# Root scales moved behind the matmuls, and the modulation sums divided between VectorE and GpSimd with ScalarE

## The chip, the core and the metric

The kernel runs on one core of a Trainium2 chip. The metric is the device time of one execution in microseconds (us). Times inside the kernel are read from one profiled execution, counted from the start of its span.

## The reference, cut to what matters

Four transformer-like layers run one after another on 512 tokens of width 1024 (the last two also on 256 context tokens). What the change touches:

```python
def rms_norm(x, g):
    y = xf * lax.rsqrt(jnp.mean(xf * xf, axis=-1, keepdims=True) + NORM_EPS)
    return (y * g).astype(x.dtype)

# first block, layers 0 and 1
h = rms_norm(x, attn_norm[0]);  q, k, v = split(h @ w_qkv)       # then attention with 8 heads
x = x + attention(...) @ w_o
x = x + swiglu(rms_norm(x, ffn_norm[l]), w_gate_up[l], w_down[l])  # (silu(g) * u) @ w_down
k, v = split(rms_norm(x, kv_norm) @ w_kv);  q = rms_norm(x, attn_norm[1]) @ w_q

# second block, layers 0 and 1: the modulation
m = silu(cond) @ w_mod + b_mod         # for cond = c and for cond = c_ctx; 6 x 1024 outputs each
h = rmsnorm(x, norm) * (1 + scale) + shift
```

`h @ w` is `root(token) * ((x * gain) @ w)`, since the root is one number for each token. `w_mod` is read once for each layer (24 MB) and serves both conditionings.

## The kernel before

The activations X lie with features on the partitions: 8 tiles of 128 features x 512 tokens. Weights come in blocks of 128 output features; each block (128 x 1024 values, 512 KB) is loaded to `w_raw`, rounded by ScalarE to `w_hi` (L568), and what rounding left is computed by VectorE as `w_lo` (L1079). Inputs are kept the same way as hi and lo. A block of a linear stage is 8 k-steps of three matmuls of 512 columns (L1679 to L1681: hi*hi, hi*lo, lo*hi), so 24 matmuls (18 where it has 6 k-steps). Four blocks use four PSUM slots in turn. The first two blocks of a stage are multiplied as a pair, k-step by k-step, so the stage starts only when `w_lo` of both is there.

Each engine runs a program written out by hand, in order; semaphores join them. A plan of stages sets it: norm, heads (attention of layer 0), the residual product `da_wo`, norm, feed-forward 0 (parts with 16, 8, 16, 8, 12, 8 blocks: up, down, up, down, up, down), norm, `kv`, norm, `q` with attention of layer 1, `sw_wo`, norm, feed-forward 1, then the second block. In a linear stage VectorE and ScalarE go block by block: first "ahead" (hi on ScalarE, lo on VectorE, of the block three further on), then the evacuation of the finished block.

A **norm** stage waits for the sums of squares (ScalarE squares each finished tile, L624; VectorE adds them, L1137), multiplies them on TensorE with ones (L1699), takes the mean on VectorE (L1003), the power -0.5 on GpSimd (L475), spreads the roots over the partitions by TensorE (L1689), and then makes for each of 8 tiles `X * gain * root` (VectorE L1308), its hi (ScalarE L714) and its lo (VectorE L1302). The second norm before `q` reuses the roots with another gain.

An up block of the **feed-forward**: the even block of a pair holds the gate, ScalarE applies silu to it out of PSUM (L636); VectorE multiplies the odd block with it (L1157), ScalarE makes the hi (L640), VectorE the lo (L1144).

The **modulation** runs beside the two feed-forwards of the first block. `w_mod` comes in 48 tiles of 128 x 1024 for each layer (SP L420, three buffers, queued between the weight loads L426 on the same SP queue). For each tile GpSimd multiplies by silu(c) and by silu(c_ctx) (L485, one buffer `mod_p` for each), and ScalarE sums each product along its row (L553). Three tiles go with every group of four blocks, in 16 of 17 groups.

At the **opening** x is loaded whole, VectorE computes the angles of the rotary tables, then the first head's weights are rounded, then the norm runs; TensorE starts its first projection behind it. A head's projection of one token tile is 24 matmuls of 384 columns (L1796 to L1798).

## Time and profile before

| | us |
|---|---|
| median of 3 runs | 3075.73 |
| lowest, highest | 3073.27, 3077.53 |
| the profiled execution, its own time | 3078.21 |
| its span | 3076.3 |

| engine | busy, share of the span |
|---|---|
| TensorE (PE) | 91% |
| VectorE (DVE) | 55% |
| ScalarE (ACT) | 41% |
| GpSimd (POOL) | 21% |

TensorE is busy nearly throughout, so its idle stretches and the stretches at a lower clock are where time can be won. The profiled execution took 2.5 us more than the median. A row of the timeline has the start, the duration, engine, line, operation and operands, how many instructions are merged, and in brackets the idle time of the engine in front of it with what ended it.

### The profile page before, as it was taken

The page shows a single profiled execution, that of the slowest core. Times are in us where ns is not written, and L with a number is a line of the kernel's source. Part 1 is how long each engine was busy: PE and PEld are TensorE (multiplying, and loading weights), DVE is VectorE, ACT ScalarE, POOL GpSimd, SP SyncE. Part 2 cuts the span into 40 slices and gives each one's busy share as a digit, 9 for nine tenths or more (in the row PEclk, how much of TensorE's full clock was granted, in tenths as well). Part 3 has the DMA queues.
Part 4 walks back from the last instruction along what each step waited for, and adds up shares of the span by engine and source line. Part 5 has one row for each costly group of instructions (what it writes and reads, how often), then busy time and mean ns, then how long its engine had stood idle before and what let it go on. Part 6 is the DMA issues. An engine that isn't in the chain of part 4 may idle for free.

```text
span 3076.3 us, 41620 instructions
## 1 busy us (share of the span) xinstructions
PE 2794.8 (91%) x14244; PEld 2339.8 (76%) x14244; DVE 1682.3 (55%) x2544; ACT 1269.5 (41%) x2121; POOL 639.8 (21%) x298
## 2 busy tenths in 40 slices
PE   4989899998687899997987899999997899899998
PEld 4777687886576778886875788888886887688886
DVE  5776534445665443435996465254455455464645
ACT  3444365654366365654211233132233466352422
POOL 0111077874011087873000000000000000000000
PEclk9999899998799999998997899999998999999999
DMA  3111244543100245443110111122111000222221
GB/s 122 42 44 60 82 157 158 177 157 117 42 19 25 82 171 175 163 162 103 55 52 31 55 55 61 56 69 69 61 36 55 28 29 8 69 89 89 96 94 63
DMA packets 67905, 252.07 MB, mean 82 GB/s; under 512 B 7456, under 2 KB 8736, under 8 KB 64928
## 3 DMA queue, kind: packets, MB, share of 16 engines
q1 hardware_dynamic: 67744, 249.99, 23.8%
q8 instruction: 93, 1.52, 0.2%
q14 instruction: 68, 0.56, 0.1%
HBM read 247.87 MB, written 2.10 MB: 81 GB/s over the span
## 4 chain that ended last, share of the span: by engine, by line
PE 45%; issue 21%; DVE 19%; POOL 7%; ACT 5%; DVEq 2%; ACTq 1%; DMA 0%; POOLq 0%
PE psum L1680 11%; PE psum L1681 11%; PE psum L1679 11%; POOL mod_p L485 7%; DVE work L1203 4%; DVE w_lo L1079 2%; PE psum L2035 2%; DVE work L1308 1%; ACT work L870 1%; ACT w_hi L568 1%; PE psum L1818 1%; DVE hx_lo L1302 1%; ACT sw_pt L882 1%; PE psum L1689 1%; PE psum L1796 1%
## 5 line engine op out<-in xcount | busy, mean ns | idle before, releaser
L1079 DVE TENSOR_TENSOR w_lo<-w_raw,w_hi 128x1024 fp32r<-128x1024 f32 (+3 forms) x334 | 447.8, 1341 | 415.8 <-ACT w_hi L568 403.5
L1679 PE MATMUL psum<-hx_hi,w_hi 128*128 128x512 f32 x1568 | 623.6, 398 | 29.6 <-DVE w_lo L1079 14.3
L1680 PE MATMUL psum<-hx_lo,w_hi 128*128 128x512 f32 x1568 | 625.1, 399 | 0.0
L1681 PE MATMUL psum<-hx_hi,w_lo 128*128 128x512 f32 x1568 | 623.7, 398 | 0.0
L485 POOL TENSOR_TENSOR mod_p<-mod_w,mod_c 128x1024 f32<-128x1024 f32 x192 | 547.6, 2882 | 186.7 <-ACT mod_p L553 150.8
L568 ACT ACTIVATE w_hi<-w_raw 128x1024 fp32r<-128x1024 f32 (+3 forms) x334 | 356.3, 1067 | 271.3 <-PE psum L1681 214.9
L475 POOL TENSOR_TENSOR tok_r<-tok_ms,half 128x4 f32<-128x4 f32 (+1 forms) x70 | 71.8, 1026 | 1857.7 <-DVE tok_ms L1003 1245.2
L1679 PEld LDWEIGHTS psum<-hx_hi,w_hi 128*128 128x128 f32 x1568 | 297.0, 189 | 80.6 <-issue 16.6
L1681 PEld LDWEIGHTS psum<-hx_hi,w_lo 128*128 128x128 f32 x1568 | 296.9, 189 | 70.4
L1680 PEld LDWEIGHTS psum<-hx_lo,w_hi 128*128 128x128 f32 x1568 | 297.6, 190 | 48.8
L1679 PE MATMUL psum<-a_hi,w_hi 128*128 128x512 f32 (+1 forms) x656 | 233.9, 357 | 19.4 <-DVE a_lo L1144 10.6
L553 ACT ACTIVATE mod_p<-mod_p 128x1024 f32<-128x1024 f32 x192 | 202.6, 1056 | 94.2 <-POOL mod_p L485 79.0
L1680 PE MATMUL psum<-a_lo,w_hi 128*128 128x512 f32 (+1 forms) x656 | 234.6, 358 | 0.0
L1681 PE MATMUL psum<-a_hi,w_lo 128*128 128x512 f32 (+1 forms) x656 | 234.0, 357 | 0.0
L1679 PE MATMUL psum<-o_hi,w_hi 128*128 128x512 f32 x544 | 217.4, 400 | 9.0 <-DVE o_lo L1609 3.9
L1680 PE MATMUL psum<-o_lo,w_hi 128*128 128x512 f32 x544 | 215.9, 397 | 0.0
L1681 PE MATMUL psum<-o_hi,w_lo 128*128 128x512 f32 x544 | 215.8, 397 | 0.0
L1166 DVE SCALAR_TENSOR_TENSOR work<-psum,vec,work 128x511 f32<-128x511 f32 (+1 forms) x132 | 83.2, 658 | 161.6 <-ACT work L654 153.6
L654 ACT ACTIVATE work<-psum,vec 128x768 f32<-128x768 f32 (+1 forms) x88 | 70.1, 796 | 220.7 <-PE psum L1681 212.1
L1130 DVE SCALAR_TENSOR_TENSOR X<-psum,mods,X 128x512 f32<-128x512 f32 x96 | 60.6, 659 | 179.6 <-PE psum L1681 178.1
L1679 PEld LDWEIGHTS psum<-a_hi,w_hi 128*128 128x128 f32 x656 | 125.0, 191 | 39.9 <-DVE a_lo L1144 11.1
L1680 PE MATMUL psum<-hc_lo,w_hi 128*128 128x256 f32 x512 | 144.3, 282 | 0.0
(263 smaller groups left out, 4954.4 us busy)
## 6 DMA issues: line engine op xcount, KB each, us to landing
mod_w<-in_w_mod SPq DMA_DIRECT2D x96, 512.0 KB, 3.6
w_raw<-in_fup SPq DMA_DIRECT2D x88, 512.0 KB, 4.6
w_raw<-in_cup SPq DMA_DIRECT2D x88, 512.0 KB, 3.5
w_raw<-in_fdown SPq DMA_DIRECT2D x32, 512.0 KB, 4.6
w_raw<-in_cdown SPq DMA_DIRECT2D x32, 512.0 KB, 3.5
w_raw<-in_da_qkv SPq DMA_DIRECT2D x8, 1536.0 KB, 6.4
w_raw<-in_fdown SPq DMA_DIRECT2D x16, 384.0 KB, 4.6
w_raw<-in_cdown SPq DMA_DIRECT2D x16, 384.0 KB, 3.0
```

The source lines that it names most:

```text
L475: pool.tensor_tensor(tok_r[:, a:b], tok_ms[:, a:b], half[:, a:b], ALU.pow).then_inc(done, 1)
L485: pool.tensor_tensor(mod_p[:, c, :], mod_w[:, u, :], mod_c[:, c, :], ALU.mult)\
L553: act.activation(mod_p[:, c, :], mod_p[:, c, :], ACT.Copy, accum_out=mods[:, layer, c, bass.ds(n, 1)]).then_inc(s_moda, 1)
L568: act.activation(w_hi[:, off:off + n], w_raw[:, raw:raw + n], ACT.Copy).then_inc(s_hi, 1)
L654: act.activation(wk[:, s, 0:toks], ps_of(st, s, 0, toks), ACT.Copy, scale=vec[:, bass.ds(b + col, 1)]).then_inc(s_ctap, 1)
L1079: dve.tensor_tensor(w_lo[:, off:off + n], w_raw[:, raw:raw + n], w_hi[:, off:off + n].bitcast(F32), ALU.subtract).then_inc(s_lo, 1)
L1166: dve.scalar_tensor_tensor(dst[:, a + 1:e], src(a, e - 1), prev, dst[:, a + 1:e], ALU.mult, ALU.add)
L1203: dve.scalar_tensor_tensor(acc, u[:, j:j + n], w, acc, ALU.mult, ALU.add)
L1679: pe.matmul(dst, wh, xh, start=first, stop=False)
L1680: pe.matmul(dst, wh, xl, start=False, stop=False)
L1681: return pe.matmul(dst, wl, xh, start=False, stop=last)
L2035: r = pe.matmul(pb[:, 5, 0:256], v_cols(tiles[k], g, p % 2), sw_pt[:, n % 2, 256 * i:256 * i + 256], start=p % 2 == 0 and k == 0, stop=p % ...
```

## The change

- **Roots behind products.** In layer 0's and 1's norms nothing waits for the root any more. The residual stage in front makes hi and lo of `X * gain` for each tile as soon as it is finished ("feed"). TensorE goes straight from the residual product to the next stage, sums the squares within it, and the root is applied at the evacuation: in heads, `kv` and `q` by ScalarE's `scale` (tokens on partitions); in the feed-forward by two more VectorE operations for each pair of up blocks with the spread root `root_b` (the gate out of PSUM times root before silu, silu(gate) times root before the product). ScalarE's silu now waits for VectorE. For `kv` and `q` the gain goes into the weights, in 8 pieces of 256 columns for hi and for lo, and one set of inputs serves both.
- **Opening.** x and the first head's weights are loaded in 8 pieces each, rounded and multiplied k-step by k-step for all four token tiles. Angles and tables move from VectorE to GpSimd, whose first root stands behind them. Two projections of the second head stand ahead of the first attention slots.
- **Modulation.** VectorE multiplies and sums for c in one instruction per tile (`accum_out`), after each block's evacuation; GpSimd multiplies and ScalarE sums for c_ctx alone, with one buffer `mod_p`. Four tiles in four buffers go with each group of four blocks, in the first 12 groups. The load of a tile waits for both users of its buffer.

```diff
-    norm(gain="ffn_norm0", toks=SEQ)
-    ffn("ffn", 0, SEQ, "f", SEQ)
-    norm(gain="kv_norm", toks=SEQ)
-    add("kv", 2, w="sw_kv", tag="a", ctx=False)
-    norm(gain="attn_norm1", toks=SEQ, again=True)
-    add("q", 4, w="sw_q", tag="a", ctx=False)
+    norm(toks=SEQ, late=True, spread=True)
+    ffn("ffn", 0, SEQ, "f", SEQ, feed="none")
+    norm(toks=SEQ, late=True)
+    add("kv", 2, w="sw_kv", tag="a", ctx=False, wgain="kv_norm")
+    add("q", 4, w="sw_q", tag="a", ctx=False, wgain="attn_norm1")
...
             def load_mod(layer, n, slot, g):
                 if not (isinstance(g, int) and g == 0):
-                    sp.wait_ge(s_modp, 96 * layer + 2 * n - 4)
+                    sp.wait_ge(s_modp, MOD_TILES * layer + n - 3)
+                    sp.wait_ge(s_modd, MOD_TILES * layer + n - 3)
...
             def modulation(layer):
                 pool.wait_ge(s_cact, layer + 1)
-                with pool.Fori(0, MOD_TILES // 3) as i:
-                    for u in range(3):
-                        for c in range(2):
-                            pool.wait_ge(s_moda, 6 * i + (96 * layer + 2 * u + c + 1))
-                            pool.tensor_tensor(mod_p[:, c, :], mod_w[:, u, :], mod_c[:, c, :], ALU.mult)\
+                with pool.Fori(0, MOD_TILES // 4) as i:
+                    for u in range(4):
+                        pool.wait_ge(s_moda, 4 * i + (MOD_TILES * layer + u + 1))
+                        pool.tensor_tensor(mod_p[:], mod_w[u], mod_c[:, 1, :], ALU.mult).then_inc(s_modp, 1)
...
+            angles()
+            head_tables()
...
+                if st["kind"] == "ffn" and st.get("late"):
+                    act.wait_ge(s_rb, st["late"]["norm0"] + 1)
+                    act.activation(root_b[:], ps_lin(3, 0, SEQ), ACT.Copy).then_inc(s_rbs, 1)
...
                     if s % 2 == 0:
-                        act.wait_ge(s_mm, b + (st["block0"] + 1))
-                        act.activation(wk[:, s // 2, 0:toks], ps_of(st, s, 0, toks), ACT.Silu).then_inc(s_gate, 1)
+                        act.wait_ge(s_gsc, q + (st["gate0"] + 1))
+                        act.activation(wk[:, s // 2, 0:toks], wk[:, s // 2, 0:toks], ACT.Silu).then_inc(s_gate, 1)
...
+                def mod(s, i):
+                    dve.wait_ge(s_cact, layer + 1)
+                    dve.scalar_tensor_tensor(mod_dump, mod_w[s].rearrange("p (a n) -> p a n", a=4), 1.0,
+                                             mod_c[:, 0, :].rearrange("p (a n) -> p a n", a=4), ALU.mult, ALU.mult,
+                                             accum_out=mods[:, layer, 0, bass.ds(n, 1)]).then_inc(s_modd, 1)
...
+                def feed(b):
+                    dve.wait_ge(s_hhi, st["feed0"] + b + 1)
+                        r = dve.scalar_tensor_tensor(hx_lo[:, b, :], X[:, b, 0:SEQ], vcol(st["feed"], b), hi,
+                                                     ALU.mult, ALU.subtract)
...
                     if s % 2 == 0:
+                        dve.tensor_tensor(gate, ps_of(st, s, 0, toks), root_b[:], ALU.mult).then_inc(s_ev, 1)
+                        dve.memset(ratio[:, 3:4], 0.0).then_inc(s_gsc, 1)
                         return
+                    dve.wait_ge(s_gate, q + (st["gate0"] + 1))
+                    dve.scalar_tensor_tensor(gate, gate, 1.0, root_b[:], ALU.mult, ALU.mult)
...
             def linear(st):
-                pair(st, st.get("ready", 0), st["k"])
+                if st["src"] == "H" and st.get("late"):
+                    pair(st, 0, 6)
+                    sum_squares(st["late"])
+                    pair(st, 6, 8)
+                    spread_roots(st["late"])
```

VectorE in an up stage with modulation, one group of four blocks, before (line 1079 is lo of the weights, 1157 the product with the gate, 1144 its lo):

```order
L1079 TENSOR_TENSOR w_lo<-w_raw,w_hi 128x1024 x2
L1157 TENSOR_TENSOR work<-psum,work 128x512
L1144 TENSOR_TENSOR o_lo<-work,o_hi 128x512
L1079 TENSOR_TENSOR w_lo<-w_raw,w_hi 128x1024 x2
L1157 TENSOR_TENSOR work<-psum,work 128x512
L1144 TENSOR_TENSOR o_lo<-work,o_hi 128x512
```

The same engine and place in the changed kernel, two blocks of the four (1207 is lo of the weights, 1232 the modulation's product with its sum):

```order
L1207 TENSOR_TENSOR w_lo<-w_raw,w_hi 128x1024
L1333 TENSOR_TENSOR work<-psum,root_b 128x512
L1335 MEMSET ratio 128x1
L1232 SCALAR_TENSOR_TENSOR work,mods<-mod_w,mod_c 128x4x256
L1207 TENSOR_TENSOR w_lo<-w_raw,w_hi 128x1024
L1338 SCALAR_TENSOR_TENSOR work<-work,root_b 128x512
L1341 TENSOR_TENSOR work<-psum,work 128x512
L1320 TENSOR_TENSOR o_lo<-work,o_hi 128x512
L1232 SCALAR_TENSOR_TENSOR work,mods<-mod_w,mod_c 128x4x256
```

Five instructions more for two blocks, and each of the two modulation products stands between an evacuation and the next lo of weights.

ScalarE at the same place, before and then changed (568 and 670 hi of the weights, 636 and 746 silu, 553 and 651 the modulation's sum, 640 and 750 hi of the product):

```order
L568 ACTIVATE w_hi<-w_raw 128x1024
L636 ACTIVATE work<-psum 128x512
L553 ACTIVATE mod_p,mods<-mod_p 128x1024 x2
L568 ACTIVATE w_hi<-w_raw 128x1024
L640 ACTIVATE o_hi<-work 128x512
L553 ACTIVATE mod_p,mods<-mod_p 128x1024 x2
```

```order
L670 ACTIVATE w_hi<-w_raw 128x1024
L746 ACTIVATE work<-work 128x512
L651 ACTIVATE mod_p,mods<-mod_p 128x1024
L670 ACTIVATE w_hi<-w_raw 128x1024
L750 ACTIVATE o_hi<-work 128x512
L651 ACTIVATE mod_p,mods<-mod_p 128x1024
```

One sum stands where two stood, now in every block, and silu reads what VectorE wrote instead of PSUM.

## Rows read from the trace of the kernel before

**Rows 1.** Page, engines: busy us, share, instructions.
```profile
PE 2794.8 (91%) x14244; PEld 2339.8 (76%) x14244; DVE 1682.3 (55%) x2544; ACT 1269.5 (41%) x2121; POOL 639.8 (21%) x298
```

**Rows 2.** Busy time by stretch: the two feed-forwards, from residual's end to their end.
```profile
365.50:748.30 382.80, 375.76 (x1601) 301.16 (x1600) 169.53 (x157) 209.96 (x319) 273.94 (x97) 0.99 0.45 158
1046.70:1432.10 385.40, 376.92 (x1600) 302.22 (x1600) 163.91 (x157) 210.86 (x318) 275.71 (x97) 0.98 0.46 158
```

**Rows 3.** Timeline of TensorE at the first feed-forward's boundary, then at full clock.
```profile
367.69 0.49 PE L1699 MATMUL psum<-ones,work 128*128 128x1 f32 x3 [2.17 <-DVE work L1137]
...
374.71 0.77 PE L1679 MATMUL psum<-hx_hi,w_hi 128*128 128x512 f32 x1 [2.56 <-DVE hx_lo L1302]
...
344.82 0.40 PE L1681 MATMUL psum<-o_hi,w_lo 128*128 128x512 f32 x1
345.05 0.39 PE L1679 MATMUL psum<-o_hi,w_hi 128*128 128x512 f32 x1
```

**Rows 4.** Timeline of TensorE before kv's first turn, q, feed-forward 1 and the second block.
```profile
793.18 1.12 PE L1920 MATMUL psum<-ident,kv_tmp 128*128 128x128 f32 x4 [10.06 <-DVE kv_tmp L1502]
...
820.96 0.55 PE L1954 MATMUL psum<-w_hi,hx_hi 128*128 128x256 f32 x1 [6.94 <-DVE hx_lo L1302]
...
1056.68 0.77 PE L1679 MATMUL psum<-hx_hi,w_hi 128*128 128x512 f32 x1 [2.56 <-DVE hx_lo L1302]
...
1442.49 0.80 PE L1699 MATMUL psum<-ones,work 128*128 128x1 f32 x3 [10.41 <-DVE work L1137]
```

**Rows 5.** Timeline of TensorE in the opening: first projection, first turn, third slot.
```profile
36.30 0.66 PE L1796 MATMUL psum<-w_hi,hx_hi 128*128 128x384 f32 x1 [13.98 <-DVE hx_lo L1302]
...
59.54 0.69 PE L1806 MATMUL psum<-ident,da_qk 128*128 128x128 f32 x2 [6.80 <-DVE da_qk L1349]
...
81.95 0.91 PE L1818 MATMUL psum<-da_T 64*128 64x384 f32 x2
```

**Rows 6.** Timeline of GpSimd, then ScalarE, then VectorE around a modulation product.
```profile
436.76 5.76 POOL L485 TENSOR_TENSOR mod_p<-mod_w,mod_c 128x1024 f32<-128x1024 f32 x2 [3.33 <-ACT mod_p L553]
...
436.59 1.05 ACT L553 ACTIVATE mod_p<-mod_p 128x1024 f32<-128x1024 f32 x1
...
437.63 1.04 ACT L568 ACTIVATE w_hi<-w_raw 128x1024 fp32r<-128x1024 f32 x1
...
445.64 0.60 ACT L636 ACTIVATE work<-psum 128x512 f32<-128x512 f32 x1 [0.22 <-issue]
...
438.71 1.54 DVE L1079 TENSOR_TENSOR w_lo<-w_raw,w_hi 128x1024 fp32r<-128x1024 f32 x1 [2.98 <-ACT w_hi L568]
...
451.53 1.23 DVE L1079 TENSOR_TENSOR w_lo<-w_raw,w_hi 128x1024 fp32r<-128x1024 f32 x1 [4.52 <-ACT w_hi L568]
...
479.80 3.48 DVE L1079 TENSOR_TENSOR w_lo<-w_raw,w_hi 128x1024 fp32r<-128x1024 f32 x1 [0.46 <-ACT w_hi L568]
```

**Rows 7.** Groups of instructions by line (page): busy, mean ns, idle before.
```profile
L485 POOL TENSOR_TENSOR mod_p<-mod_w,mod_c 128x1024 f32<-128x1024 f32 x192 | 547.6, 2882 | 186.7 <-ACT mod_p L553 150.8
```

**Rows 8.** Timeline of VectorE: a product of 384 columns, then the evacuation of an odd block.
```profile
88.12 0.62 DVE L1364 SCALAR_TENSOR_TENSOR work<-work,ratio 128x384 f32<-128x384 f32 x1
...
440.58 0.69 DVE L1157 TENSOR_TENSOR work<-psum,work 128x512 f32<-128x512 f32 x1 [0.34 <-issue]
```

**Rows 9.** Timeline of ScalarE and VectorE between feed-forward 0 and kv.
```profile
747.96 1.91 ACT L568 ACTIVATE w_hi<-w_raw 128x2048 fp32r<-128x2048 f32 x1 [1.34 <-DMA w_raw<-in_sw_kv]
...
775.27 1.45 DVE L1460 MEMSET sw_va<- 128x1664 f32 x1 [0.47 <-issue]
...
790.14 0.42 DVE L1318 TENSOR_REDUCE tok_ms<-kv_tmp 128x4 f32<-128x256 f32 x1
```

**Rows 10.** Timeline of VectorE at feed-forward 1's last residual block.
```profile
1439.88 0.69 DVE L1127 TENSOR_TENSOR X<-psum,X 128x512 f32<-128x512 f32 x1
```

**Rows 11.** GpSimd's small operations by line: busy us, mean ns, idle before.
```profile
L475 POOL TENSOR_TENSOR tok_r<-tok_ms,half 128x4 f32<-128x4 f32 x66 | 66.5, 1008 | 943.3 <-DVE tok_ms L1003 573.8 <-DVE tok_ms L1320 369.5
L518 POOL COPY inv_wide<-inv 128x256 f32<-128x256 f32 x32 | 20.2, 631 | 381.1 <-DVE inv L1597 381.1
```

More of the change, by code:

```diff
@@ L59, in make_plan @@
     stages = []
-    n = dict(block=0, lin=0, tile=0, gate=0, conv=0, norm=0, hset=0, rms=0)
+    n = dict(block=0, lin=0, tile=0, gate=0, conv=0, norm=0, hset=0, rms=0, ht=0)
     loads = [0, 0, 0, 0]
@@ L274, in program @@
         s_cact = sem("c_act_ready")
[L275 removed]
+        s_modl = [sem(f"mod_loaded{u}") for u in range(4)]
         s_modp = sem("mod_products")
         s_moda = sem("mod_summed")
+        s_modd = sem("mod_first_summed")
         s_trig = sem("trig_args_ready")
@@ L490, in _ @@
                     modulation(st["mod"][0])
-                if st["kind"] == "norm" and not st.get("again"):
+                if st["kind"] == "norm":
                     root(0, st["toks"] // P, s_ms, st["rms0"] + 1, s_pw)
@@ L784, in slot @@
                         turned(j + 3, i - 1, 1 - par)
-                split(st, 1, 1, 1)
-                for t in range(4):
-                    evac_proj(t, t, 0)
-                    if t:
-                        turned(t - 1, t - 1, 0)
+                evac_proj(0, 0, 0, first=True)
+                evac_proj(1, 1, 0, first=True)
+                constants()
+                for t in range(3):
+                    turned(t, t, 0)
+                    if t < 2:
+                        evac_proj(t + 2, t + 2, 0, first=True)
                 for i in range(4):
@@ L951, in _ @@
                 if k == "norm":
-                    if not st.get("final"):
+                    if not st.get("final") and not st.get("late"):
                         norm(st)
@@ new lines, in _ @@
+            add_first(KT_D - 1)
+            means(stages[0])
+            for part in range(3):
+                if part < 2:
+                    dve.wait_ge(s_whi0, KT_D + part)
+                else:
+                    dve.wait_ge(s_hi, 2)
+                cols = slice(3 * D + D * part, 4 * D + D * part)
+                r = dve.tensor_tensor(w_lo[:, cols], second_raw[:, D * part:D * part + D], w_hi[:, cols].bitcast(F32),
+                                      ALU.subtract)
+            r.then_inc(s_lo, 1)
@@ L1281, in norm @@
                 toks = st["toks"]
-                if not st.get("again") and st is not stages[0]:
+                if st is not stages[0]:
                     means(st)
+                if st.get("late"):
+                    return
                 dve.wait_ge(s_rb, st["norm0"] + 1)
@@ L1658, in _ @@
                 if k == "norm":
-                    if st["gain"] == (0, 0):
+                    if st.get("gain") == (0, 0):
                         modulation()
@@ L1769, in linear @@
             def linear(st):
-                pair(st, st.get("ready", 0), st["k"])
+                if st["src"] == "H" and st.get("late"):
[3 more added lines that the diff above has]
+                    spread_roots(st["late"])
+                else:
+                    pair(st, st.get("ready", 0), st["k"])
                 for s in (2, 3):
@@ L1859, in slot @@
                         turn_outputs(h - 1)
-                    if more:
+                    if more and not (first and i < 2):
                         project(j + 4, i, 1 - par, h + 1)
@@ L1932, in kv @@
                         .then_inc(S["kpj"], 1)
+                    if n == 0 and st.get("late"):
+                        sum_squares(st["late"])
                     if 2 <= n <= nt:
@@ L2081, in _ @@
                 if k == "norm":
-                    norm(st)
+                    if not st.get("late"):
+                        norm(st)
                     hset[0] += 0 if st.get("final") else 1
```

477 lines of the change are left out of this document (322 added, 155 removed).

## The prediction

> **What bounds the kernel now.** I read the page's engine table first: TensorE is busy 91% of the span, the next engine 55% [rows 1]. Then the busy time by stretch: from the end of the residual product in front of it to its own end, the first feed-forward takes 382.8 us and the second 385.4, TensorE busy for about 376 of either [rows 2]. Then TensorE's timeline: at full clock one matmul of 512 columns follows another after 0.23 us [rows 3]; over a long run 0.2335, so a block of 24 takes 5.6 us and one of 18 takes 4.2. A feed-forward has 60 of the first and 8 of the second: 60 x 5.6 + 8 x 4.2 = 369.8. The 13.0 us left in the first are 9.2 at its head (365.52 to 374.71 [rows 3]), 2.5 for the lower clock behind that pause, and about 1 of short waits. So VectorE, ScalarE and GpSimd keep up in the feed-forwards today, and a gain in the middle of them is not to be had: only boundaries can be shortened. The question is whether the three still keep up after the change.
>
> The other pauses of TensorE that the change touches are the opening (first projection at 36.30, third slot's scores at 81.95 [rows 5]), the way into kv and q (10.06 in front of the first turn, 6.94 in front of q's first matmul [rows 4]) and the end of feed-forward 1 (10.41 [rows 4]).
>
> **The change part by part: modulation.** VectorE and GpSimd disturb each other already. Alone, lo of the weights takes 1.23 us (at 451.53). At 438.71 it takes 1.54 while a GpSimd product begun at 436.76 is running; two products take 5.76 with that lo between them, and 5.76 - 1.23 = 4.53 = 2 x 2.27: lo ends exactly 1.23 after the end of the first product (436.76 + 2.27 + 1.23 = 440.26; it ended at 440.25), and the second product starts only then. At 479.80 lo takes 3.48 [rows 6], which is 1.23 and one product of 2.25. So the two instructions are done one after the other and never together, and GpSimd's mean of 2.88 us [rows 7] is 2.27 and waiting. VectorE's operations with PSUM show nothing of it: 0.69 for the product with the gate [rows 8].
>
> Today GpSimd has two buffers, so that a product may start while ScalarE sums the other, and three tiles go with four blocks. Afterwards there is one buffer, so GpSimd and ScalarE take turns, one tile goes with each block, and VectorE has its own product. That product reads two operands of 1024 values in SBUF as lo does: I take 1.3 us (0.62 for 384 columns [rows 8] would give 1.65 with no fixed part taken out; 1.23 is lo's), and that it too is done apart from GpSimd's. No row shows that pair of operations: its nearest row is lo's.
>
> The Trainium skill (SBUF — State Buffer, "SBUF: two separate sides") describes a port pair that VectorE and GpSimd share as a lock held for a whole instruction, and has a two-input VectorE operation and a GpSimd operation on SBUF exclude each other. Lo's rows agree; it would extend this to the new product, which is the assumption above; without it a feed-forward would come to about 407 us instead of 425.
>
> One pair of up blocks, followed from the end of ScalarE's sum of an odd tile (0): VectorE is in its product of that tile until 1.1; GpSimd's product 2.3, to 3.4; lo of weights 1.3 with its handoff, to 4.7; gate times root 0.7 and the memset, to 5.5; silu 0.6 [rows 6] and its handoff, to 6.2; ScalarE's sum 1.05 [rows 6], to 7.3 (the even tile's VectorE product lies beside these two); GpSimd 2.3, to 9.6; lo, to 10.9; silu times root 0.8, to 11.8; product with the gate 0.7 [rows 8], to 12.5; hi 0.6, to 13.2; sum 1.05, to 14.3. Nothing is idle by chance in this ring: each step waits for the one before. **14.3 us for a pair against TensorE's 11.2**.
>
> An up part has 8 pairs. Lo of block 3 is ready 17.5 us into the stage (c is loaded 5 us after its start, then the exponent table, silu of c and the copy of the roots are ahead of it on ScalarE), and lo of block 17, which the down part's first pair needs, at 17.5 + 7 x 14.3 = 117.6. TensorE would be there at 9 + 15 x 5.6 = 92.6, less the pause saved, so it loses about 25. In the down part a block costs the engines lo 1.3, VectorE's product 1.3, an evacuation 0.7, GpSimd's 2.3 and handoffs, 5.6 to 6.1, so nothing is caught up; the second up part loses 8 x 3.1 = 25 and 2 at the change of parts: 27. From group 12 of 17 on there is no modulation and no loss. The longer waits let the clock fall now and then: 1. **Feed-forward: 369.8 + 25 + 27 + 1 + the head of the stage.** At its head the 9.2 and the slow clock go, and sums 1.1 and a spread of the roots 1 remain inside the stage: 2. That is 425: **+42 in the first, +40 in the second**. Bounds: 385 if nothing of it bites; 407 if only lo shares (the ring loses its first 1.1: 13.2 per pair, 17 + 18 lost); 455 at the rival of half rate below.
>
> **Boundaries.** Into kv: today VectorE works on the norm until 775, then memset, tables and split until 790.1 (775.27 to 790.14 [rows 9], 14.9 us), then the turn at 793.18. With the norm gone VectorE starts these when the residual ends; what then comes last is the load and its rounding: the load is there at 747.96 and hi takes 1.91 [rows 9], now in 8 pieces for hi and for lo, +1. I take the first turn at 780 (-13), and q without its 6.94 and its copies: -7.5; pieces +1. **-19.5**, between -15 and -23. Into the feed-forwards: counted above. End of feed-forward 1: TensorE ends at 1432.09 and VectorE's last evacuation at 1439.88 [rows 10] because the last blocks (4.2 us) are faster than their modulation; without modulation in the last part the 10.41 comes down to the 3.1 of such a boundary elsewhere: **-7**.
>
> **Opening.** X and the weights now come in 8 pieces, and each is 12 matmuls of 384 columns, 12 x 0.17 = 2.1 us, double that at half clock. From the first piece (some 8 us) with the first 12 us at half clock the projection ends near 29 instead of 53. ScalarE has three operations for each piece, about 1.6 us: no bound. Squares, sums and means are ready near 30, but GpSimd now has 23 operations for angles and 19 for the tables in front of its first root. A copy of 256 columns is 0.63, a power 1.01 [rows 11]; at 0.63 or below, 42 of them end by 30 and the root is there at 31 to 36; the first turn comes at 37 to 42 (59.54 today) and the third slot at 53 to 60 (81.95) [rows 5]. **-25**, between -28 and -22; with 1.0 for each operation the root comes near 45 and only -10 is left.
>
> Sum: 42 + 40 - 19.5 - 7 - 25 = **+30.5**, rounded. Against the profiled execution's 3078.2: 3108.7. That execution stood 2.5 above the median, so the prediction is **3106 us**.
>
> **The rivals.** *Faster: the new product doesn't exclude GpSimd's, or the ring has play that I don't see.* For it: only lo has been seen to wait; VectorE's 55% leaves room. Against it: the new product has lo's operands. With 407 instead of 425 the sum is 3106 - 36 = 3070; if the feed-forward hides all, at 385 each, 3106 - 80 = **3026**. A feed-forward may cost 384 + 51.5 / 2 = 410 before the boundaries' gain is used up; 15 us of it hang on each us of the ring, so it decides at a ring of 13.3. Chance 0.15.
>
> *Slower still: VectorE's product with its accumulated sum runs at half rate,* 2.5 us for 1024 values. The ring grows by 1.2 for the odd tile and about 0.5 for the even, 16.0 for a pair: 14 us more in each up part, 455 in all for a feed-forward, **3166**. The row at 88.12 [rows 8] is a product of two SBUF operands at 1.6 ns per column, against which half rate would be seen, but it accumulates nothing. Chance 0.13. The Trainium skill (Vector Engine (DVE) Microarchitecture Reference, "Points that are easy to get wrong") has this operation at half throughput when both sources are in SBUF and not bf16; the row at 88.12, 0.62 for 384 columns, is slower per column than lo (1.2 ns), which by itself leaves the rule open.
>
> *The opening gives 10, not 25,* since GpSimd's operations are the path: **3121**. Chance 0.10.
>
> **How the numbers follow.** The forecast, 0.62, gives 3106; its own bounds (ring 13.9 to 14.7, boundaries as above) are 3080 to 3130. The range reaches down into the faster rival's cases, to 3056, and up past the opening's rival to 3150; outside lie the half rate at its full price and the fully hidden modulation. A measurement of this kernel tells 0.2%, 6 us, from no change. Faster by more 0.17, within 0.07, slower by more 0.76.
>
> **What would show it.** Right: the feed-forward's stretch near 425; in its up parts TensorE waits about 3 us per pair for lo of the weights; lo takes 2.3 or more where it meets a GpSimd product, and VectorE's product with the sum does so too; the last up part has no such waits; the first turn of kv near 780 plus what came before, the third slot at 53 to 60. Wrong: a stretch under 410 (the product shares with GpSimd), a mean of 2.5 us for that product also where GpSimd is idle (half rate), a root after 40 us in the opening.

## The result, and the profile after

The changed kernel takes 3124.6 us (median, 3124.24 to 3125.23) against 3075.7; the ratio is 1.0162, with a 95% interval of 1.0149 to 1.0174: slower, by 1.6%. The forecast was 3106, range 3056 to 3150. Its profiled execution has a span of 3123.4, which is 47.1 more than the 3076.3 of before. By stretch, from TensorE's timeline in both:

| stretch | before | after | difference | forecast |
|---|---|---|---|---|
| opening and heads, to the end of `da_wo` | 365.5 | 348.3 | -17.2 | -25 |
| feed-forward 0 | 382.8 | 429.4 | +46.6 | +42 |
| `kv`, `q`, `sw_wo` | 298.4 | 281.2 | -17.2 | -19.5 |
| feed-forward 1 | 385.4 | 428.7 | +43.3 | +40 |
| pause at its end | 10.4 | 4.0 | -6.4 | -7 |
| second block | 1633.8 | 1631.8 | -2.0 | 0 |

The engines, and the two feed-forwards as rows (start:end, length, then PE, PEld, DVE, ACT and POOL busy, the granted clock, DMA share, GB/s); they answer to [rows 1, 2]:

```profile
PE 2809.1 (90%) x14220; PEld 2344.2 (75%) x14220; DVE 1920.2 (61%) x2834; ACT 1186.2 (38%) x1972; POOL 377.0 (12%) x244
...
348.30:777.70 429.40, 388.71 (x1604) 306.70 (x1602) 296.23 (x312) 161.87 (x230) 129.97 (x49) 0.96 0.42 142
1058.90:1487.60 428.70, 387.72 (x1601) 305.83 (x1599) 298.78 (x310) 160.83 (x220) 129.67 (x49) 0.96 0.43 145
```

VectorE is busy 296 us of the 429, not full. Yet TensorE waits for it. TensorE's timeline, at the waits in front of four pairs of blocks and in front of the two down parts (all for lo of the weights, L1207):

```profile
380.39 0.49 PE L1865 MATMUL psum<-hx_hi,w_hi 128*128 128x512 f32 x1 [1.49 <-DVE w_lo L1207]
...
395.14 0.73 PE L1865 MATMUL psum<-hx_hi,w_hi 128*128 128x512 f32 x1 [2.19 <-DVE w_lo L1207]
...
410.01 0.49 PE L1865 MATMUL psum<-hx_hi,w_hi 128*128 128x512 f32 x1 [1.86 <-DVE w_lo L1207]
...
424.76 0.49 PE L1865 MATMUL psum<-hx_hi,w_hi 128*128 128x512 f32 x1 [2.19 <-DVE w_lo L1207]
...
468.55 0.77 PE L1865 MATMUL psum<-o_hi,w_hi 128*128 128x512 f32 x1 [8.33 <-DVE w_lo L1207]
...
629.92 0.77 PE L1865 MATMUL psum<-o_hi,w_hi 128*128 128x512 f32 x1 [6.75 <-DVE w_lo L1207]
```

From 395.14 to 424.76 are four blocks, 29.62 us: **14.8 us for a pair** of up blocks (forecast 14.3, TensorE alone 11.2). Of the 7.2 us that two pairs take beyond 22.4, TensorE is idle for 4.9 and the rest is its own work at a lower clock (busy 24.7, granted clock 0.94). One turn of the **ring** (a closed chain of steps on several engines, each of which waits for the one before), on VectorE, ScalarE and GpSimd:

```profile
410.11 0.69 DVE L1333 TENSOR_TENSOR work<-psum,root_b 128x512 f32<-128x512 f32 x1 [0.23 <-issue]
411.21 1.23 DVE L1232 SCALAR_TENSOR_TENSOR work<-mod_w,mod_c 128x1024 f32<-128x1024 f32 x1 [0.22 <-issue]
414.02 2.57 DVE L1207 TENSOR_TENSOR w_lo<-w_raw,w_hi 128x1024 fp32r<-128x1024 f32 x1 [1.58 <-ACT w_hi L670]
416.76 0.69 DVE L1338 SCALAR_TENSOR_TENSOR work<-work,root_b 128x512 f32<-128x512 f32 x1 [0.17 <-issue]
...
420.10 1.23 DVE L1232 SCALAR_TENSOR_TENSOR work<-mod_w,mod_c 128x1024 f32<-128x1024 f32 x1 [0.27 <-issue]
421.90 2.73 DVE L1207 TENSOR_TENSOR w_lo<-w_raw,w_hi 128x1024 fp32r<-128x1024 f32 x1 [0.57 <-ACT w_hi L670]
...
418.35 0.63 ACT L750 ACTIVATE o_hi<-work 128x512 f32 x1 [4.35 <-DVE work L1341]
419.21 1.06 ACT L651 ACTIVATE mod_p<-mod_p 128x1024 f32<-128x1024 f32 x1 [0.23 <-issue]
...
413.12 2.40 POOL L566 TENSOR_TENSOR mod_p<-mod_w,mod_c 128x1024 f32<-128x1024 f32 x1 [4.32 <-ACT mod_p L651]
...
420.44 3.11 POOL L566 TENSOR_TENSOR mod_p<-mod_w,mod_c 128x1024 f32<-128x1024 f32 x1 [4.92 <-ACT mod_p L651]
```

Read it from GpSimd's first row. ScalarE's sum ends at 413.0 and releases the product at 413.12; ScalarE then rounds the next weights, so lo is ready to start at 414.02, when the product has 1.5 us to go. Lo takes 2.57 where it takes 1.23 alone, and ends 1.07 behind the end of the product. At 420.44 the product is itself held by VectorE's product (3.11 for 2.40), and lo behind it takes 2.73. VectorE's product takes 1.23 when nothing holds it: it is not at half rate.

In the middle of the up parts the weights are loaded in time, but in the down parts and in the first blocks behind them ScalarE's hi waits for them. Who ScalarE waited for in feed-forward 0 (us in total, times, longest):

```profile
ACT w_hi L670 <- DMA w_raw<-in_fdown: 25.0, 8, 4.8
ACT w_hi L670 <- DMA w_raw<-in_fup: 16.2, 5, 4.2
```

In the kernel before these are 6.0 and 1.3. The last up part has the root operations and no modulation but the end of the last product:

```profile
676.71:743.70 66.99, 66.99 (x289) 53.81 (x288) 35.47 (x47) 20.10 (x25) 1.89 (x1) 1.00 0.31 92
```

Its 12 blocks take 67.0 us at full clock, which is TensorE's own pace (12 x 5.6): the root operations by themselves cost nothing there.

### The profile page after: what moved, and what is told of

It reads as the page before. It is cut to its first block, busy times and chain, and to the rows that moved or that the text cites. A ratio compares the mean times of both kernels' runs of the same rounds, so it can differ in the third digit from the quotient of the medians.

```text
span 3123.4 us, 41754 instructions
## 1 busy us (share of the span) xinstructions
PE 2809.1 (90%) x14220; PEld 2344.2 (75%) x14220; DVE 1920.2 (61%) x2834; ACT 1186.2 (38%) x1972; POOL 377.0 (12%) x244
## 4 chain that ended last, share of the span: by engine, by line
PE 51%; DVE 21%; issue 16%; ACT 6%; DVEq 2%; DMA 2%; ACTq 1%; POOL 1%; POOLq 1%; SPq 0%
PE psum L1866 13%; PE psum L1865 13%; PE psum L1867 13%; DVE w_lo L1207 5%; DVE work L1386 3%; PE psum L2253 2%; DMA w_raw<-in_fup 1%; ACT w_hi L670 1%; ACT work L997 1%; DVE work L1232 1%; PE psum L2011 1%; ACTq L672 1%; ACT sw_pt L1009 1%; PE psum L1989 1%; DVE work L1341 1%
## 5 line engine op out<-in xcount | busy, mean ns | idle before, releaser
L1865 PE MATMUL psum<-hx_hi,w_hi 128*128 128x512 f32 x1568 | 631.2, 403 | 75.6 <-DVE w_lo L1207 65.4
L1207 DVE TENSOR_TENSOR w_lo<-w_raw,w_hi 128x1024 fp32r<-128x1024 f32 (+1 forms) x328 | 498.8, 1521 | 211.1 <-ACT w_hi L670 196.4
L670 ACT ACTIVATE w_hi<-w_raw 128x1024 fp32r<-128x1024 f32 (+1 forms) x328 | 343.7, 1048 | 314.9 <-PE psum L1867 197.5
L566 POOL TENSOR_TENSOR mod_p<-mod_w,mod_c 128x1024 f32<-128x1024 f32 x96 | 257.7, 2684 | 379.9 <-ACT mod_p L651 379.9
L1865 PE MATMUL psum<-o_hi,w_hi 128*128 128x512 f32 x544 | 220.8, 406 | 35.8 <-DVE w_lo L1207 30.2
L1232 DVE SCALAR_TENSOR_TENSOR work<-mod_w,mod_c 128x1024 f32<-128x1024 f32 x96 | 157.0, 1635 | 17.2 <-issue 15.6
L1865 PEld LDWEIGHTS psum<-o_hi,w_hi 128*128 128x128 f32 x544 | 104.9, 193 | 63.4 <-DVE w_lo L1207 31.8
## 6 DMA issues: line engine op xcount, KB each, us to landing
w_raw<-in_fdown SPq DMA_DIRECT2D x16, 384.0 KB, 3.0
w_raw<-in_cdown SPq DMA_DIRECT2D x16, 384.0 KB, 3.0
```

The lines of the kernel that those rows point to most:

```text
L566: pool.tensor_tensor(mod_p[:], mod_w[u], mod_c[:, 1, :], ALU.mult).then_inc(s_modp, 1)
L670: r = act.activation(w_hi[:, off:off + n], w_raw[:, raw:raw + n], ACT.Copy)
L1207: r = dve.tensor_tensor(w_lo[:, off:off + n], w_raw[:, raw:raw + n], w_hi[:, off:off + n].bitcast(F32), ALU.subtract)
L1232: dve.scalar_tensor_tensor(mod_dump, mod_w[s].rearrange("p (a n) -> p a n", a=4), 1.0, mod_c[:, 0, :].rearrange("p (a n) -> p a n", a=4), ...
L1865: pe.matmul(dst, wh, xh, start=first, stop=False)
```

## The experiments

Each ratio is to the kernel before, run again beside the experiment (medians 3074.8, 3078.0 and 3080.9). "Stretch" is feed-forward 0. "Count" and "load" theory both say that VectorE simply has too many instructions; nothing in them is about the loads of weights.

**1. The modulation as before, in the changed kernel.**

```diff
-                        pool.tensor_tensor(mod_p[:], mod_w[u], mod_c[:, 1, :], ALU.mult).then_inc(s_modp, 1)
+                        for c in range(2):
+                            pool.wait_ge(s_moda, 6 * i + (96 * layer + 2 * u + c + 1))
+                            pool.tensor_tensor(mod_p[c], mod_w[u], mod_c[:, c, :], ALU.mult).then_inc(s_modp, 1)
...
-                    dve.scalar_tensor_tensor(mod_dump, mod_w[s]..., accum_out=mods[:, layer, 0, bass.ds(n, 1)])
```

> The changed kernel with the modulation as before: GpSimd multiplies for c and for c_ctx, ScalarE sums both, three tiles for four blocks in 16 groups, two product buffers; roots behind products and the new opening stay. Ring theory (one product buffer, GpSimd and ScalarE taking turns, VectorE's lo and product kept apart from GpSimd's product, 14.8 us for a pair): no ring, GpSimd's six products per group are 13.8 us and held 4.9 by lo, under TensorE's 22.4, so a feed-forward stretch is 374 to 380 us and the span 3123.4 - 2 x 52 + 6.5 for the late end of feed-forward 1, near 3026. Root theory (the slow part is gate times root in front of silu): the ring stays over 11.2, the stretch over 400, the span over 3070. Load theory (VectorE has too many instructions): as the ring theory, 374 to 380.

3192.6 us, ratio 1.0381 (1.0364 to 1.0398), and feed-forward 0 takes 459.2: slower than both kernels. Both the ring theory as I then had it and the load theory had 374 to 380 here; of the expectations only the root theory's bounds (over 400, over 3070) held. In the changed kernel, then, the modulation's change is not what is dear. GpSimd's rows, VectorE's silu times root, and VectorE's group of that line in feed-forward 0:

```profile
428.47 2.41 POOL L564 TENSOR_TENSOR mod_p<-mod_w,mod_c 128x1024 f32<-128x1024 f32 x1 [8.17 <-ACT mod_p L650]
430.84 3.37 POOL L564 TENSOR_TENSOR sw_vb<-mod_w,mod_c 128x1024 f32<-128x1024 f32 x1
...
432.14 2.62 DVE L1321 SCALAR_TENSOR_TENSOR work<-work,root_b 128x512 f32<-128x512 f32 x1 [0.18 <-issue]
...
L1321 DVE SCALAR_TENSOR_TENSOR work<-work,root_b 128x512 f32<-128x512 f32 x22 | 58.3, 2648 | 3.3 <-issue 2.7
```

Two products now start behind each pair of sums. Lo meets the end of the first, silu times root the second: 2.65 us on average for 0.69 of work, in all 22 pairs. And here, unlike in the kernel before, silu of the next pair can't start until VectorE is through. Beside the root operations, the modulation of the change loses less than the old one.

**2. The modulation's change alone, in the kernel before.**

```diff
+                    dve.scalar_tensor_tensor(mod_dump, mod_w[s]..., 1.0, mod_c[:, 0, :]..., ALU.mult, ALU.mult,
+                                             accum_out=mods[:, layer, 0, bass.ds(n, 1)]).then_inc(s_modd, 1)
...
-                            pool.tensor_tensor(mod_p[:, c, :], mod_w[:, u, :], mod_c[:, c, :], ALU.mult)
+                        pool.tensor_tensor(mod_p[:], mod_w[u], mod_c[:, 1, :], ALU.mult)
```

> The kernel before with the modulation's part of the change alone: VectorE multiplies and sums for c, GpSimd and ScalarE do c_ctx with one buffer, four tiles in four buffers, first 12 groups. Ring theory: the ring of 14.8 us loses gate times root, the memset and silu times root (0.7 + 0.1 + 0.8), 13.1 us a pair against 11.2, so a feed-forward stretch is 382.8 + 15 x 1.9 - 3 = 408, and the span 3076.3 + 2 x 25 - 6.5 = 3120. Load theory: VectorE's instructions are 7.1 us a pair, no bound, stretch 383, span 3070. Root theory: nothing of the root is in it, stretch 383, span 3070.

3114.4 us, ratio 1.0129 (1.0112 to 1.0146), stretch 404.4, a pair 12.4. So the modulation's change loses 21.6 by itself, in the kernel of before. Load and root theory had 383 here and fail; the ring theory's price without the root operations (408, 13.1) was a little high.

```profile
365.20:769.60 404.40, 381.68 (x1600) 302.80 (x1600) 266.85 (x254) 162.54 (x223) 142.86 (x49) 0.97 0.45 151
```

But this run has a second path that the ring theory doesn't have. SP may load a tile only when VectorE has multiplied the one before it in that buffer, and the next weights are queued behind that load. Here SP's two loads behind a product of VectorE that ended at 425.08, the hi that waits for the second, and all such waits of the stretch in up parts (1.3 us in the kernel before):

```profile
425.22 0.33 SPq L424 DMA_DIRECT2D mod_w<-in_w_mod  x1
425.81 0.33 SPq L430 DMA_DIRECT2D w_raw<-in_fup  x1
...
429.89 1.06 ACT L569 ACTIVATE w_hi<-w_raw 128x1024 fp32r<-128x1024 f32 x1 [1.28 <-DMA w_raw<-in_fup]
...
ACT w_hi L569 <- DMA w_raw<-in_fup: 37.6, 20, 6.0
```

How much of the 21.6 hangs on these late loads and how much on products that hold each other, no run separates.

**3. GpSimd's product cut to 64 columns.**

```diff
-                        pool.tensor_tensor(mod_p[:], mod_w[u], mod_c[:, 1, :], ALU.mult).then_inc(s_modp, 1)
+                        pool.tensor_tensor(mod_p[:, 0:64], mod_w[u][:, 0:64], mod_c[:, 1, 0:64], ALU.mult).then_inc(s_modp, 1)
...
-                act.activation(mod_p[:], mod_p[:], ACT.Copy, ...
+                act.activation(mod_p[:], mod_c[:, 1, :], ACT.Copy, ...
```

> The changed kernel with GpSimd's modulation product cut from 1024 to 64 columns; ScalarE sums 1024 columns of c_ctx in its place, so that its time stays (the sums for c_ctx are left out of what is computed). VectorE's instructions are all there. Ring theory: the two 2.3 us of GpSimd and what they hold up go, ring near 10, stretch 373 to 377, span 3123.4 - 2 x 54 = 3015. Load theory (VectorE itself too full) and root theory: stretch stays at 425 to 430, span 3115 to 3123.

3052.4 us, ratio 0.9927 (0.9910 to 0.9943), stretch 393.1. Of the 56 us lost (429.4 against 373, which is 369.8 and 3 at its head), 36 hang on GpSimd's product. Load and root theory had 425 to 430, so they fall as single causes; but the ring theory's 373 to 377 was also missed, by 16. TensorE's waits repeat every 12.5 us:

```profile
401.21 0.49 PE L1865 MATMUL psum<-hx_hi,w_hi 128*128 128x512 f32 x1 [0.37 <-DVE w_lo L1207]
...
413.69 0.49 PE L1865 MATMUL psum<-hx_hi,w_hi 128*128 128x512 f32 x1 [0.66 <-DVE w_lo L1207]
...
426.26 0.49 PE L1865 MATMUL psum<-hx_hi,w_hi 128*128 128x512 f32 x1 [0.37 <-DVE w_lo L1207]
...
404.71 1.06 ACT L670 ACTIVATE w_hi<-w_raw 128x1024 fp32r<-128x1024 f32 x1 [0.48 <-DMA w_raw<-in_fup]
```

GpSimd's short product is no step of that ring: hi 1.06, lo 1.3, gate times root 0.8, silu 0.7, sum 1.25, hi 1.06, lo 1.3, silu times root 0.75, product 0.75, hi 0.7, sum 1.25, in all 10.9, and 0.5 to 0.9 more where hi waits for its weights to be loaded (the last row), and handoffs. **Without that wait for the load the two pairs are 12.0 and 11.7: ScalarE and VectorE alone, each waiting for the other, come out a little over 11.2.** That is worked out from the rows; no run takes the wait for the load away. In the kernel before silu read PSUM and waited for TensorE alone.

**4. Two product buffers for GpSimd.**

```diff
-                        pool.tensor_tensor(mod_p[:], mod_w[u], mod_c[:, 1, :], ALU.mult).then_inc(s_modp, 1)
+                        pool.tensor_tensor(mod_p[u % 2], mod_w[u], mod_c[:, 1, :], ALU.mult).then_inc(s_modp, 1)
```

> The changed kernel with two product buffers for GpSimd in place of one, used in turn, nothing else. Ring theory: a product no longer waits for the sum before it; what is left is time that GpSimd and VectorE can't share: per pair 2 x 1.23 lo, 2 x 1.3 products, 0.7 silu times root, 0.7 lo of the product and 2 x 2.3 of GpSimd, 11.1, with handoffs 11.2 to 12: stretch 375 to 390, span 3015 to 3050. If the sum of excluded work and not the turns with ScalarE sets the 14.8 (exclusion theory: PSUM operations are held up too, 13.2 or more): stretch over 400, span over 3065. Load and root theories: unchanged, 429 and 3123.

3123.6 us, ratio 1.0158 (1.0141 to 1.0174): no change, stretch 429.5. The ring theory as I had written it, with the single buffer in it, is wrong. The rows say why: with two buffers both are full, and each product still starts when a sum frees one.

```profile
417.13 1.06 ACT L652 ACTIVATE sw_vb<-sw_vb 128x1024 f32<-128x1024 f32 x1 [0.23 <-issue]
418.10 0.19 ACT L652 ACTIVATION_READ_ACCUMULATOR sw_vb<-sw_vb  x1
...
418.36 3.12 POOL L567 TENSOR_TENSOR sw_vb<-mod_w,mod_c 128x1024 f32<-128x1024 f32 x1 [4.92 <-ACT sw_vb L652]
...
419.83 2.73 DVE L1208 TENSOR_TENSOR w_lo<-w_raw,w_hi 128x1024 fp32r<-128x1024 f32 x1 [0.57 <-ACT w_hi L671]
```

The product is in the ring not because ScalarE waits for it (it doesn't) but because the end of each sum starts one, a microsecond or a little more before lo. I call this the coupling theory: silu waits for VectorE, the sum stands behind silu, its end starts the product that holds the next lo, and lo is what silu's input waits behind.

**5. VectorE's product cut to 64 columns.**

```diff
-                    dve.scalar_tensor_tensor(mod_dump, mod_w[s].rearrange("p (a n) -> p a n", a=4), 1.0,
+                    dve.scalar_tensor_tensor(mod_dump[:, 0, 0:64], mod_w[s][:, 0:64], 1.0,
```

> The changed kernel with VectorE's modulation product cut from 1024 to 64 columns (the sums for c are left out of what is computed); GpSimd's product, ScalarE's sum and the root operations stay. First theory, refined by the two-buffer run (the ring runs through end of ScalarE's sum, GpSimd's product that it releases, lo held behind that product, gate times root, silu, sum): only the 1.1 us of VectorE's product that delay GpSimd's on odd tiles go, the ring is 13.7, the stretch 429 - 15 x 1.1 = 412, the span 3123.4 - 2 x 17 = 3090. Rival, that VectorE's own product is what overloads the feed-forward: the stretch falls to 375 to 385, span under 3035.

3102.3 us, ratio 1.0083 (1.0066 to 1.0100), stretch 418.8, a pair 14.1 (two waits at 392.88 and 407.02). VectorE's 48 products of 1.63 are worth 11 us only: most of each lies beside silu and the sum. The rival (375 to 385) fails, and the refined theory's 13.7, 412 and 3090 were missed too (span 3099.7). It took off the 1.1 that the product reaches past the sum; what it costs GpSimd's product is 3.11 - 2.40 = 0.7, and 14.8 - 0.7 is the 14.1 measured.

**6. Another order.** ScalarE sums ahead of silu or hi, VectorE multiplies ahead of lo.

```diff
+                            mod(s, i)
                             evac(4 * i + s, s, i)
-                            mod(s, i)
...
+                            mod(s, i)
                             ahead(s, i)
                             evac(4 * i + s, s, i)
-                            mod(s, i)
```

> The changed kernel in another order, nothing left out or added: in each block ScalarE sums the modulation product ahead of its silu or hi (it stood behind), and VectorE multiplies for the modulation ahead of lo of the weights (it stood behind the evacuation). Coupling theory (silu waits for VectorE behind lo, and the sum behind silu releases the GpSimd product that holds the next lo): the sum leaves the ring, and of GpSimd's two products one only still holds silu times root, which reads two operands in SBUF: ring near 13.3, stretch 403 to 410, span near 3123 - 2 x 23 = 3077. Count theory (so many instructions on VectorE and ScalarE for a pair, whatever their order): nothing changes, stretch 429, span 3123.

3078.4 us, ratio 1.0000 (0.9991 to 1.0010), stretch 402.8, a pair 13.1, as the coupling theory had it; with the same instructions, so the count theory falls. Two things moved at once, and no run has one without the other: ScalarE's sum left the ring, and VectorE's product, now ahead of lo, is what meets GpSimd's (2.01 at 406.44), so that lo takes 1.23 on both sides of it (at 403.89 and 408.62). VectorE's earlier product also lets SP load earlier: ScalarE's waits for loads of weights fall from 41.2 us to 1.7. These lie in the down parts and just behind them; the pair's 14.8 has none. What is still held is silu times root (GpSimd, VectorE, and VectorE's group in feed-forward 0):

```profile
409.68 2.43 POOL L566 TENSOR_TENSOR mod_p<-mod_w,mod_c 128x1024 f32<-128x1024 f32 x1 [2.31 <-ACT mod_p L651]
...
410.01 2.64 DVE L1338 SCALAR_TENSOR_TENSOR work<-work,root_b 128x512 f32<-128x512 f32 x1 [0.17 <-issue]
...
L1338 DVE SCALAR_TENSOR_TENSOR work<-work,root_b 128x512 f32<-128x512 f32 x22 | 35.3, 1607 | 3.3 <-issue 2.8
```

**7. That order, and silu's result in PSUM.**

```diff
-                        act.activation(wk[:, s // 2, 0:toks], wk[:, s // 2, 0:toks], ACT.Silu).then_inc(s_gate, 1)
+                        act.activation(ps_of(st, s, 0, toks), wk[:, s // 2, 0:toks], ACT.Silu).then_inc(s_gate, 1)
...
-                    dve.scalar_tensor_tensor(gate, gate, 1.0, root_b[:], ALU.mult, ALU.mult)
+                    dve.tensor_tensor(gate, ps_of(st, s - 1, 0, toks), root_b[:], ALU.mult).then_inc(s_ev, 1)
```

> As the run before in the same order, and silu writes its result to the gate's own PSUM bank, so that silu times root reads PSUM and root_b where it read two operands in SBUF; the bank is given back one evacuation later. Coupling theory: no step of the ring is then held by GpSimd's product but lo, ring under TensorE's 11.2, stretch 372 to 380, span 3123 - 2 x 54 = 3015. If operations with an operand in PSUM are held by GpSimd too: as the run before, 403 to 410. Count theory: 429.

**3023.2 us, ratio 0.9819 (0.9803 to 0.9835)**: faster than both kernels. The stretches are 376.3 and 381.1 (the second a little over what was expected). The expectation still had lo held; here lo isn't either (1.26 us on average for 128 x 1024). The same product of GpSimd, the same step beside it, and its group:

```profile
425.00 2.50 POOL L566 TENSOR_TENSOR mod_p<-mod_w,mod_c 128x1024 f32<-128x1024 f32 x1 [2.24 <-ACT mod_p L651]
...
425.40 0.69 DVE L1338 TENSOR_TENSOR work<-psum,root_b 128x512 f32<-128x512 f32 x1 [0.16 <-issue]
...
L1338 DVE TENSOR_TENSOR work<-psum,root_b 128x512 f32<-128x512 f32 x22 | 15.2, 691 | 3.3 <-issue 2.7
347.40:723.70 376.30, 373.96 (x1604) 300.03 (x1602) 252.35 (x312) 165.23 (x230) 145.95 (x49) 1.00 0.48 162
```

**8. The change without its feed-forward part.** Norms in front of the feed-forwards, silu out of PSUM and modulation as before; opening, heads, `kv` and `q` as changed. The part of the edit for the norms:

```diff
-    norm(toks=SEQ, late=True, spread=True)
+    norm(gain="ffn_norm0", toks=SEQ)
...
-    norm(toks=SEQ, late=True, spread=True)
+    norm(gain="ffn_norm1", toks=SEQ)
```

> The kernel before in everything of the feed-forwards (norm in front, silu out of PSUM, modulation on GpSimd and ScalarE, three tiles, 16 groups); of the change it keeps the opening and the roots behind heads, kv and q. If the boundaries' gains are their own and what the change loses lies in the feed-forwards alone: opening -17, kv and q -17, feed-forwards 383 and 385 as before, late end of feed-forward 1 as before, span 3076.3 - 35 = 3041. If part of the boundaries' gain came out of the new modulation (feed-forward 0 ending without sums): kv and q less, span 3045 to 3052.

3050.4 us, ratio 0.9915 (0.9898 to 0.9931), span 3044.3; feed-forwards 385.5 and 384.0. So what the change loses lies in the feed-forwards, and most of the boundaries' gain is their own. Not all: the profiled execution was the lowest of four, and the median fits the second expectation (3045 to 3052). The way from feed-forward 0 to feed-forward 1 gains 10.9 here, not 17.2; TensorE waits 6.66 for lo of kv's weights at 738.05 (2.55 in the changed kernel). That a last part without modulation gives the rest is the likely reason, not tested by itself.

**9. Silu's result in PSUM, in the changed kernel's own order** (the edit of 7, without that of 6).

> The changed kernel in its own order, with silu's result in the gate's PSUM bank so that silu times root reads no two operands in SBUF; nothing else. In the changed kernel silu times root takes 0.69 on average, so it is not held there (lo is, at 2.12). Coupling theory: nothing is won as long as the sum stands behind silu: stretch 427 to 431, span 3121 to 3125. If silu times root's second SBUF operand is costly by itself (for GpSimd's product, say): stretch 415 or less, span under 3095.

3122.5 us, ratio 1.0137 (1.0122 to 1.0153), stretch 430.0: nothing, as expected. The PSUM operand pays only where a product of GpSimd meets that step.

**10. The kernel of 7 with two repairs more.** GpSimd's first root between the tables of two token tiles; on the way from `kv` to `q` the last key tile is evacuated ahead of the split of q's second piece.

```diff
+                    if t == 2:
+                        root(0, stages[0]["toks"] // P, s_ms, stages[0]["rms0"] + 1, s_pw)
...
-                split(st["after"], 1, 1)
                 turned(nt - 1)
+                split(st["after"], 1, 1)
...
-                split(st["after"], 1, 1)
                 k_low(nt - 1)
+                split(st["after"], 1, 1)
```

> The run with sum first and silu in PSUM (span 3024.4), and two repairs more. In the opening GpSimd does its first root between the tables of the second and the third token tile, where the means are ready at 30.1 and the root came at 37.2: the root at 31 to 32, the second head's projection and the first turn 4 to 6 us earlier. On the way from kv to q the last key tile is taken out of PSUM (ScalarE, then VectorE) ahead of the split of q's second weight piece and not behind it: the 7.86 in front of q's first projection falls to 4 or less, and the same in the second block, 5.3 today. Span 3024.4 - 5 - 4 - 2 = 3013. If the opening is held by lo of the second head (4.23 us from 30.2) the first repair gives 3 only; if q then waits for its own weights the second gives under 2: span 3018.

**3016.6 us, ratio 0.9785 (0.9770 to 0.9801)**, span 3014.8. Its root, the second head's first projection, the third slot and q's first projection:

```profile
29.13 1.04 POOL L508 TENSOR_TENSOR tok_r<-tok_ms,half 128x4 f32<-128x4 f32 x1 [0.66 <-DVE tok_ms L1123]
...
33.34 0.66 PE L1991 MATMUL psum<-w_hi,hx_hi 128*128 128x384 f32 x1 [3.33 <-DVE w_lo L1166]
...
57.45 1.64 PE L2013 MATMUL psum<-da_T 64*128 64x384 f32 x2
...
772.99 0.36 PE L2174 MATMUL psum<-w_hi,hx_hi 128*128 128x256 f32 x1 [1.73 <-issue]
```

The root comes at 30.2 (37.2 in the changed kernel), the third slot 5.7 us earlier than there, and the pause in front of q falls from 7.86 to 1.73. Of the 7.0 at the root, 1.1 were there before it: the means came at 29.0, not at 30.1. At the end of `da_wo` 3.5 of the 5.7 are left. In the end it is 9.6 us of span between the two profiled executions, where 11 were expected; the medians are 6.6 apart.

## Why the prediction came out as it did, point by point

**The sign and the mechanism of the feed-forward held.** The forecast's ring has every step that the rows show, in their order; it was 14.3 us and is 14.8. What was too small is ScalarE's sum: from the end of silu (or of hi) to the end of the sum it is 1.38 us, a pause of 0.23 in front and the reading of the accumulator (0.18) behind, where 1.1 was taken, twice. The other terms cancel: GpSimd's product 2.40 for 2.3, but lo ends 1.07 behind it, not 1.3. With 15 us of stretch to each us of ring, 0.5 is 7.5, and 4.6 and 3.3 of it showed. By the forecast's terms the first down part starts 116.6 us into the stage, the second 161.4 behind it, and 145.6 are left; the trace has 120.3, 161.4 and 147.8. So the longer ring shows in the first up part only; why it doesn't in the second was not looked for. That VectorE's product and GpSimd's exclude each other was an assumption, and it held (3.11 at 420.44), as did its 1.3 us (1.23 and 0.08 for the accumulator). The trace agrees with the rule of the Trainium skill that the prediction cited for it (SBUF — State Buffer, "SBUF: two separate sides").

**Terms that were wrong without being needed.** "385 if nothing of it bites" doesn't follow from the prediction's own terms, which give 369.8 + 1 + 2 = 373; experiment 7 came to 376.3 and 381.1. The fully hidden rival's time should have been 3002, not 3026. "9 + 15 x 5.6" is 93.0, not 92.6, and what has to be set against 117.6 is 2 + 16 x 5.6 = 91.6, so the first up part loses 26 by its own ring, not 25. And the down part was priced by VectorE's and GpSimd's work, 5.6 to 6.1 for a block; the trace has 5.4 (hi at 485.04 and, four blocks later, at 506.46), with hi waiting for its load each time, a wait that the prediction put at nothing.

**Half rate didn't occur.** L1232 takes 1.23 for 1024 columns with two SBUF operands and an accumulated sum, the same as lo. The rule cited from the Trainium skill (Vector Engine (DVE) Microarchitecture Reference, "Points that are easy to get wrong") is not borne out by this row.

**What was wrong in the reading of it.** The step "Afterwards there is one buffer, so GpSimd and ScalarE take turns" is not a cause: with two buffers the time is the same (experiment 4). And the loss stood under the modulation. By the runs it is neither part alone: modulation's change by itself loses 21.6 of the 46.6 (experiment 2), the root operations by themselves nothing (the last up part, 67.0 us for 12 blocks), and the root operations with the old modulation 30 more than with the new (experiment 1). The root operations make silu wait for VectorE, and with modulation beside them that ties ScalarE, VectorE and GpSimd into one ring; with GpSimd's product cut short it is still 12.5, of which 0.5 to 0.9 are the load (experiment 3). The diff's sentence "ScalarE's silu now waits for VectorE" was the one to weigh; the prediction has that wait in its ring, but only as one hop of 0.6 us, under the heading of modulation.

**The faster rival** (407 or less) did not come; it decided at a ring of 13.3. Experiment 6, with 13.1, is close to that edge, and its ratio to the kernel before is 1.000.

**The opening: -17.2, not -25.** The step that failed is GpSimd's queue. The means were ready at 30.1, as forecast, and that was partly luck: 12 us of TensorE's slow pace were taken and 4.6 came (8.09 to 12.7), and later waits for lo of the pieces (1.73 in front of 24.77) filled part of the difference. The root came at 37.2 (31 to 36 forecast), since GpSimd's table operations stood in front of it and took up to 1.43 where others of the same kind took 0.45. They ran beside VectorE's lo of the second head's weights. VectorE, GpSimd, GpSimd's root, and the second head's projection that waits for it:

```profile
29.98 0.16 DVE L1121 TENSOR_SCALAR tok_ms<-psum 128x4 f32<-128x4 f32 x1 [1.15 <-PE psum L1886]
30.23 4.23 DVE L1164 TENSOR_TENSOR w_lo<-second_raw,w_hi 128x1024 fp32r<-128x1024 f32 x3
...
29.11 0.45 POOL L556 TENSOR_TENSOR da_tab_s<-work,trig 128x128 f32<-128x128 f32 x1
...
31.96 1.43 POOL L556 TENSOR_TENSOR da_tab_s<-work,trig 128x128 f32<-128x128 f32 x1
36.17 1.04 POOL L508 TENSOR_TENSOR tok_r<-tok_ms,half 128x4 f32<-128x4 f32 x1 [0.16 <-issue]
...
38.46 0.69 PE L1989 MATMUL psum<-w_hi,hx_hi 128*128 128x384 f32 x1 [7.35 <-ACT da_v L844]
63.16 1.65 PE L2011 MATMUL psum<-da_T 64*128 64x384 f32 x2
```

The third slot's scores came at 63.2 (53 to 60 forecast, 81.95 before), and behind the pauses TensorE ran at 1.2 GHz (granted clock 0.50 from 56 to 70 us). The end of `da_wo` came between 345.9 and 348.4 in kernels with the same opening, so 1 to 2 us of this term is not to be told from chance. Experiment 10 shows the queue as the cause of most of it: with the root in another place the third slot comes 5.7 earlier, at 57.45, inside the forecast.

**`kv` and `q`: -17.2 for -19.5.** The first turn came 29.1 us behind the end of feed-forward 0 (44.9 before), 3 better than the forecast (31.7). But the 6.94 in front of q was not gone: it is 7.84. What was late next is the evacuation of the last key tile, on VectorE behind the eight pieces of q's second split:

```profile
832.90 3.26 DVE L1215 SCALAR_TENSOR_TENSOR w_lo<-w_raw,vec,w_hi 128x256 fp32r<-128x256 f32 x8 [5.87 <-ACT w_hi L667]
836.25 0.69 DVE L1661 TENSOR_TENSOR sw_k<-psum,sw_k 64x512 fp32r<-64x512 f32 x1
...
837.05 0.55 PE L2172 MATMUL psum<-w_hi,hx_hi 128*128 128x256 f32 x1 [7.84 <-issue]
```

Experiment 10, where that evacuation stands ahead of the split, has 1.73 there. Part of this gain came with the feed-forward's part of the change, by the run without it (experiment 8).

**The end of feed-forward 1** went from 10.41 [rows 4] to 3.95 as forecast. The second block's -2.0 was not forecast; it is spread over small pauses, and its cause was not looked for.

## What to carry to other kernels

When an edit makes one in-order engine wait for another that already waits for it, write the whole ring down, with every engine that the end of a step releases, and compare it with the pace of the bound; the busy shares (VectorE 69% here, 296 of 429 us) don't show it. Ask the same of the loads that wait for the moved work (experiment 2). Look at what an operation's end starts on a third engine: here moving ScalarE's sum ahead of silu and VectorE's product ahead of lo, at the same count of instructions, won 46 us. And a step that two engines can't do together may be moved out of the way by where its operand lies.

## What the runs showed of the hardware

- VectorE operations with two operands in SBUF are held by a running GpSimd product, to its end: lo 2.57 for 1.23, silu times root 2.65 on average for 0.69 (experiment 1). With one operand in PSUM they are not: 0.69 on average in the same place (experiments 6 and 7). The hold works the other way too: GpSimd's product takes 3.11 for 2.40, and its 128 x 128 operations 1.43 for 0.45.
- A product of two SBUF operands with an accumulated sum takes 1.23 us for 1024 columns, as long as lo without one, and 0.08 for the accumulator; ScalarE's accumulated sum is followed by 0.18.
